# The q projection of the first head group joins the K projection between the modulation units, taken in six shares of channels

## The reference, cut to what matters

```
mod   = silu(c)     @ ada_w + ada_b      # (6 * 2048); mod_c the same with c_ctx
h     = rms_norm(x)   * norm1_g * (1 + sc1)  + sh1
hc    = rms_norm(ctx) * norm1_g * (1 + csc1) + csh1
proj  = h  @ w_in          # qa, ka, va, qb, kb, vb, gates; each of qa..vb is 1024 columns
projc = hc @ w_in          # of which keys and values are used
```

## Time and profile before

| | |
|---|---|
| median of 3 runs | 1735.7 us (1734.41 to 1738.12) |
| the profiled execution | 1735.94 us, span 1734.3 us |
| TensorE busy | 97% of the span |
| VectorE, ScalarE, GpSimd busy | 62%, 43%, 6% |
| mean transfer rate | 214 GB/s; about 387 GB/s until 130 us |
| TensorE's clock | 0.7 in the first of 40 slices of the span, full in the others |

### The profile page before, as it was taken

The page is one execution under the profiler, slowest core; times in us unless marked ns, Lnnn a source line. Parts: engine busy times, 40 slices in busy tenths (PEclk is TensorE's granted clock), DMA queues, the critical chain, the costliest instruction groups (busy, mean ns, idle before and its releaser), DMA issues.

```text
span 1734.3 us, 23809 instructions
## 1 busy us (share of the span) xinstructions
PE 1683.1 (97%) x8800; PEld 1376.4 (79%) x8800; DVE 1082.6 (62%) x1351; ACT 752.3 (43%) x960; POOL 108.7 (6%) x161
## 2 busy tenths in 40 slices
PE   4999999999999999999999999999999999999996
PEld 1468888888888678888888788888888888888885
DVE  1338777768796675554555666666666666655556
ACT  2233222623222564444444555555555555444444
POOL 0002222122121000000000000000000000000000
PEclk7999999999999999999999999999999999999999
DMA  9999988369695127566565566666666665555551
GB/s 354 386 387 334 305 298 283 77 234 333 227 323 193 51 83 261 191 190 192 188 242 190 150 184 193 186 190 191 186 191 189 187 191 186 191 194 193 194 193 62
DMA packets 161237, 371.53 MB, mean 214 GB/s; under 512 B 11607, under 2 KB 12359, under 8 KB 160022
## 3 DMA queue, kind: packets, MB, share of 16 engines
q1 hardware_dynamic: 139808, 291.98, 51.9%
q0 software_dynamic: 20144, 74.22, 12.6%
q10 hardware_dynamic: 1222, 4.47, 0.6%
HBM read 368.43 MB, written 2.21 MB: 214 GB/s over the span
## 4 chain that ended last, share of the span: by engine, by line
PE 92%; DMA 4%; DVE 2%; ACT 1%; issue 1%; SPq 0%; DVEq 0%; POOL 0%; ACTq 0%
PE ps L1838 21%; PE ps L1837 10%; PE ps L1847 10%; PE ps L1849 10%; PE ps L1848 10%; PE ps L2224 4%; PE ps L2225 4%; PE ps L2223 4%; PE ps L1762 3%; DMA raw<-in_ada_w 3%; PE ps L1764 3%; PE ps L1763 3%; PE ps L1834 1%; PE ps L1754 1%; PE ps L1916 1%; PE ps L1898 1%
## 5 line engine op out<-in xcount | busy, mean ns | idle before, releaser
L1127 DVE TENSOR_TENSOR w_lo<-raw,w_hi 128x1024 fp32r<-128x1024 f32 x480 | 584.8, 1224 | 432.9 <-ACT w_hi L669 432.5
L669 ACT CAST w_hi<-raw 128x1024 fp32r<-128x1024 f32 x480 | 503.4, 1050 | 771.3 <-PE ps L1849 273.8
L1838 PE MATMUL ps<-h2T,w_hi 128*128 128x512 f32 x1320 | 463.2, 394 | 0.0
L1837 PE MATMUL ps<-h2T,w_lo 128*128 128x256 f32 x1320 | 366.9, 278 | 0.0
L1838 PEld LDWEIGHTS ps<-h2T,w_hi 128*128 128x128 f32 x1320 | 247.9, 188 | 53.6
L1837 PEld LDWEIGHTS ps<-h2T,w_lo 128*128 128x128 f32 x1320 | 248.4, 188 | 4.2
L1847 PE MATMUL ps<-w_hi,hT 128*128 128x512 f32 x512 | 202.5, 395 | 0.0
L1849 PE MATMUL ps<-w_hi,hT 128*128 128x512 f32 x512 | 199.4, 390 | 0.0
L1848 PE MATMUL ps<-w_lo,hT 128*128 128x512 f32 x512 | 199.4, 389 | 0.0
L1201 DVE SCALAR_TENSOR_TENSOR ada_acc<-ada_raw,silu_c,ada_acc 128x512 f32<-128x512 f32 x240 | 180.0, 750 | 27.2 <-DMA ada_raw<-in_ada_w 11.5
L2223 PE MATMUL ps<-w_hi,f_hi 128*128 128x512 f32 x352 | 137.0, 389 | 1.0 <-DVE conv_in L1583 1.0
(11 more groups left out here) (224 smaller groups left out, 1917.1 us busy)
## 6 DMA issues: line engine op xcount, KB each, us to landing
raw<-in_ffn_w_up SPq DMA_DIRECT2D x176, 512.0 KB, 3.8
raw<-in_w_in SPq DMA_DIRECT2D x152, 512.0 KB, 4.7
ada_raw<-in_ada_w POOLq DMA_DIRECT2D x128, 512.0 KB, 5.9
raw<-in_ffn_w_down SPq DMA_DIRECT2D x88, 512.0 KB, 4.4
raw<-in_ada_w SPq DMA_DIRECT2D x64, 512.0 KB, 10.7
raw<-in_w_out SPq DMA_DIRECT2D x32, 512.0 KB, 3.9
raw<-in_w_branch_a SPq DMA_DIRECT2D x16, 512.0 KB, 3.7
raw<-in_w_branch_b SPq DMA_DIRECT2D x16, 512.0 KB, 3.6
```

The costliest lines, as they stand in the source:

```text
L669: act.copy(w_hi[:, s % SPLIT_SLOTS, :], raw[:, s, :]).then_inc(hi_ready[s], 1)
L1127: dve.tensor_tensor(w_lo[:, s % SPLIT_SLOTS, :], raw[:, s, :], w_hi[:, s % SPLIT_SLOTS, :], ALU.subtract).then_inc(lo_ready[s], 1)
L1837: pe.matmul(ps[:, b + t, 0:SEQ], w_lo[:, row4(s), at], high(kc), start=False, stop=False)
L1838: mm = pe.matmul(o, w_hi[:, row4(s), at], both(kc), start=False, stop=(kc == KC - 1))
```

## The change

The channels are taken in six shares of 2, 4, 4, 2, 2 and 2 groups. A share of four is as a quarter was: sixteen units, one channel group of rows and 1024 columns each. A share of two is eight units; a unit holds two channel groups of rows and 512 columns (256 of shift, 256 of scale), still 512 KB, but brought by two DMAs whose contiguous runs are 1 KB where they were 2 KB. The number of units stays 64. In a share of two the two channel groups' sums lie in different partitions, and `turn_mod` adds them by a matmul with a small matrix (`pair_sum`, made once on VectorE).

The q weights of job 1 now go through `ada_raw` too: K and q pieces alternate, sixteen in all, fourteen of them placed among the units by `KQ_LOADS`. TensorE works in chunks: a slot has six, four of K (six 512-column matmuls) and two of q (two tiles each, twelve 256-column matmuls; latent tokens only, hi*hi, hi*lo, lo*hi added in one PSUM area instead of two). 36 chunks stand among the units (`CHUNKS`), 12 behind them. The q result needs no addition on VectorE. All token groups are turned in one bank (7), which also takes `turn_mod`. Job 1 is gone from the loops of all engines; its 12 ada steps are spread over jobs 2 to 5 (41, 14, 40, 33). The copy of the K result stands in ScalarE's queue at job 2, slot 2.

```diff
-QUARTERS = 4
-SHARE = KC // QUARTERS
-K_AFTER = (3, 10)
-K_TILES = {(0, 0): (1, 6), (0, 1): (1, 8), (0, 2): (1, 10), (0, 3): (1, 12),
-           (1, 0): (1, 13), (1, 1): (1, 15), (1, 2): (2, 1), (1, 3): (2, 3),
...
+SHARES = (2, 4, 4, 2, 2, 2)
+FIRST_KC = [sum(SHARES[:q]) for q in range(len(SHARES))]
+ROWS_OF = [2 if n == 2 else 1 for n in SHARES]
+UNITS_OF = [KC // n for n in ROWS_OF]
+KQ_LOADS = {(1, 1): 0, (1, 4): 1, (1, 9): 2, (1, 13): 3, (2, 2): 4, (2, 6): 5, (2, 9): 6, (2, 12): 7,
+            (3, 1): 8, (3, 3): 9, (3, 5): 10, (4, 0): 11, (4, 4): 12, (4, 7): 13}
+KQ_CHUNKS = 6
+CHUNKS = {1: (7, 9, 11, 13, 15), 2: (1, 5, 6, 7, 8, 9, 10, 11, 12, 14, 15), 3: (1, 3, 5, 6, 7),
+          4: (0, 1, 2, 3, 4, 5, 6, 7), 5: (0, 1, 2, 3, 4, 5, 6)}
+SPLIT_BEFORE = {1: (2, 3), 2: (6, 7), 4: (12,)}
+SPLIT_BEHIND = {3: (10,), 5: (14,)}
+SPLIT_AFTER = {0: (0,), 1: (1,), 3: (4,), 5: (5,), 7: (8,), 9: (9,), 11: (11,), 12: (13,), 15: (15,)}
-ADA_BANKS = (0, 4, 5, 4)
-MOD_BANK = 6
+ADA_BANKS = [6 * (q > 0) for q in range(len(SHARES))]
+MOD_BANK = 7
+TURN_BANK = 7
-ADA_STEPS = {1: 12, 2: 34, 3: 13, 4: 37, 5: 32, 6: 24, 7: 13, 8: 28, 9: 13, 10: 32, 11: 18}
+ADA_STEPS = {2: 41, 3: 14, 4: 40, 5: 33, 6: 24, 7: 13, 8: 28, 9: 13, 10: 32, 11: 18}
...
 # SyncE, a modulation unit and a weight piece
-                    sp.dma_start(raw[:, n % SLOTS, :].rearrange("p (a n) -> p a n", a=2),
-                                 shift_scale[:, kc, :, GROUP * q:GROUP * (q + 1)]).then_inc(raw_landed[n % SLOTS], 16)
+                    for k in range(ROWS_OF[q]):
+                        sp.dma_start(dst[:, k, :, :], shift_scale[:, ROWS_OF[q] * u + k, :, cols])\
+                            .then_inc(raw_landed[n % SLOTS], 16)
...
+                    if i >= 2:
+                        sp.wait_ge(k_landed[i % 2], 16 * (i // 2))
+                    if i >= ADA_SLOTS:
+                        sp.wait_ge(lo_ready[s - 2], j + 1)
+                    sp.dma_start(ada_raw[:, i % ADA_SLOTS, :, :], w_in_v[:, 2 * s:2 * s + 2, col:col + GROUP])\
+                        .then_inc(k_landed[i % 2], 16)
...
 # TensorE
+            def head_q(s, t):
+                o, row = ps[:, 4 + t // 2, (t % 2) * SEQ:(t % 2 + 1) * SEQ], head_row(1, s)
+                for i in range(2):
+                    kc = 2 * s + i
+                    at = slice(i * GROUP + t * P, i * GROUP + (t + 1) * P)
+                    pe.matmul(o, w_hi[:, row, at], hT[:, 0, 0, kc, :], start=(kc == 0 and t % 2 == 0), stop=False)
+                    pe.matmul(o, w_hi[:, row, at], hT[:, 0, 1, kc, :], start=False, stop=False)
+                    mm = pe.matmul(o, w_lo[:, row, at], hT[:, 0, 0, kc, :], start=False,
+                                   stop=(kc == KC - 1 and t % 2 == 1))
+                return mm
...
+            for _, q, u in ADA_UNITS:
+                unit_ada(q, u)
+                if q and u == 0:
+                    turn_mod(q - 1)
+                for _ in range(CHUNKS.get(q, ()).count(u)):
+                    head_chunk(chunks)
+                    chunks += 1
+                if q:
+                    for n, behind in ((0, 1), (1, 2), (2, 4), (3, 5)):
+                        if u == behind and n < SHARES[q - 1]:
+                            turn_tokens(FIRST_KC[q - 1] + n)
+            last_pair = KQ_CHUNKS * (SLOTS - 1)
+            head_chunk(chunks)
+            turn_mod(len(SHARES) - 1)
+            head_chunk(chunks + 1)
+            turn_tokens(KC - 2)
+            head_chunk(chunks + 2)
+            turn_tokens(KC - 1)
...
-            for j in range(JOB_NA + 1, JOB_DIFF - 1):
+            for j in range(JOB_NA + 2, JOB_DIFF - 1):
                 projection(j)
```

More of the change, by code:

```diff
@@ L588, in load_ada @@
                     if skip_wait and pair < ADA_SLOTS:
-                        pool.wait_ge(lo_ready[SLOTS - ADA_SLOTS + pair], 1)
+                        pool.wait_ge(lo_ready[SLOTS - 2 + pair // 2], pair % 2 + 1)
                     else:
@@ L820, in _ @@
             last = JOB_DIFF - 1
-            for j in range(JOB_NA + 1, JOB_DIFF):
+            for j in range(JOB_NA + 2, JOB_DIFF):
                 for s in range(SLOTS):
@@ L1753, in unit_ada, with products_k @@
                 for n, at in enumerate(PIECE_AT):
+                    kc = u if SHARES[q] == 4 else 2 * u + n // 2
                     mm = pe.matmul(ps[at:at + 32, ADA_BANKS[q], 0:PIECE], c_pair[:, 2 * kc:2 * kc + 32],
-                                   raw[:, slot, n * PIECE:(n + 1) * PIECE], start=(kc == 0), stop=(kc == KC - 1))
+                                   raw[:, slot, n * PIECE:(n + 1) * PIECE], start=(u == 0),
+                                   stop=(u == UNITS_OF[q] - 1))
                 mm.then_inc(ada1_used, 1)
-            def products_k(slot, t, b, kc, i):
+            def products_k(row, t, b, kc, i):
@@ L1768, in unit_k, with head_row @@
+                pe.matmul(o, w_hi[:, row, at], hT[:, :, 1, kc, :], start=False, stop=False)
+                return pe.matmul(o, w_lo[:, row, at], hT[:, :, 0, kc, :], start=False, stop=(kc == KC - 1))
+            def unit_k(s, row, t, b):
                 for i in range(2):
-                    mm = products_k(slot, t, b, 2 * s + i, i)
+                    mm = products_k(row, t, b, 2 * s + i, i)
                 return mm
-            def head_k(s, t):
-                if t == 0:
+            def head_row(j, s):
+                return (2 * s + j) % SPLIT_SLOTS
@@ new lines, in _ @@
+            last_pair = KQ_CHUNKS * (SLOTS - 1)
[5 more added lines that the diff above has]
+            turn_tokens(KC - 1)
+            for n in range(chunks + 3, last_pair):
+                head_chunk(n)
+            take(0, SLOTS - 1)
+            for i in range(2):
+                pe.wait_ge(hT_ready, KC - 1 + i)
+                for t in range(TILES):
+                    mm = products_k(head_row(0, SLOTS - 1), t, 0, KC - 2 + i, i)
@@ L1818, in sum_mod @@
+            mm.then_inc(used[SLOTS - 1], 1)
+            for n in range(last_pair + TILES, last_pair + KQ_CHUNKS):
+                head_chunk(n)
             def sum_mod(g, j):
```

237 lines of the change are left out of this document (122 added, 115 removed), and 4 rows, old and new, of the table K_TILES.

## The result

The changed kernel takes 1740.33 us (median of 8 runs, 1738.25 to 1743.50) against 1736.74 for the kernel before on the same chips (8 runs): a ratio of 1.0022, 95% interval [1.0013, 1.0031]. The spans of the profiled executions are 1738.9 and 1734.3 us. Job 2 starts at 159.50 us instead of 155.14. What is lost is lost in the head.

A forecast was written before the change was run, and what follows sets the result against it. TensorE's own work behind the last transfer it waits for was taken as the bound: landing 66.9 plus 91.2 us puts job 2 at 158.1 against 155.14, +3.0 on 1735.94, so 1738.9 us; range 1735.5 to 1742.5.

The forecast's parts named there:

- The landing at 66.9: Share 2's unit 5 (number 29) lands at 66.9 us with TensorE there for it; no wait for transfers later.
- The work behind unit 29: TensorE's work from 66.9 us to job 2: 90.7 us, with 0.5 added 91.2, so job 2 starts at 158.1.
- the other bound: q chunks' 256-column matmuls at 0.15 us each if weight loads could not keep up: 6 us more over 16 chunks.
- the ledger's shortfall: The work ledger, checked on the kernel before, gave 72.4 us against 72.9 in the rows; 0.5 us was added.
- the stall of the second turn in share 3: With one turning bank, a turn one unit behind another waits for ScalarE's modulation: +0.6 us.
- SyncE's new waits: In the head, waits for `k_landed` and `lo_ready` may issue piece 10 up to 2 us late; cost 0.
- the K copy: Behind the last K chunk, 1.86 us, covered by the two last q chunks; uncovered it would cost up to 2.
- changing over: A chunk among the units pays about 0.2 us; for twelve q chunks among the units +2.4 us.
- VectorE late: Rival: VectorE falls behind in jobs 2 to 5, costing some 5 us, 1744 us; chance 0.20.
- Bound by transfers: Rival: transfers bound the head, job 2 at 147.3 us, 1728.1, or 1732 for half; chance 0.11 including hidden idle time.
- 256-column matmuls by their weight loads: Rival: weight loads limit the q chunks' matmuls, +6 us on the forecast, 1745 us; chance 0.06.
- 1 KB runs as 2 KB ones: Rival: in shares of two, 1 KB packets take as long as 2 KB ones; job 2 at about 185, 1766 us; chance 0.03.

The follow-up runs named there:

- e6b: The kernel before with the six shares alone, q left as job 1, tokens turned two units ahead; job 2 at 159.44 us, ratio 1.0027 to the kernel before.
- e1: The changed kernel with its chunks two at a time from share 2 on; job 2 at 157.65 us, ratio 1.0012 to the kernel before.
- e7: q joined as in the changed kernel, but four shares of four groups and chunks in pairs; job 2 at 154.69 us, ratio 0.9994 to the kernel before.
- e10: The changed kernel with chunks in pairs and one 2 KB-run transfer per unit in shares of two; job 2 at 156.14 us, ratio 0.9997 to the kernel before.
- e11: e7 with ten chunks in share 1, token turns moved and splits placed anew; job 2 at 153.90 us, ratio 0.9990 to the kernel before.
- e8: e7 with the token turns spread and the old slot's chunks between them; job 2 at 157.18 us, ratio 1.0004 to the kernel before.
- e9: e8 with the chunks three at a time; job 2 at 159.48 us, ratio 1.0008 to the kernel before.
- e3b: The changed kernel, units of shares of two by one 128-partition transfer with 2 KB runs, other columns; job 2 at 157.81 us, ratio 1.0013 to the kernel before.

## Why the prediction was right, and where not

**Time and side.** +3.0 us was predicted; it is +4.4 at job 2 and +3.6 at the medians. 1740.33 lies in the forecast's own range (1735.5 to 1742.5) and on the side forecast. The forecast called this "within" 3.5 us of the kernel before; the medians lie 3.6 us apart, just outside that, and the interval of the ratio is clear of 1. The forecast's mechanism, TensorE's own work behind the last transfer that it waits for, is what the trace shows. Of the 1.4 us at job 2 between 158.1 and 159.50, 0.4 were there at unit 29 and 1.0 came in behind it.

**The landings.** 1.53 us was worked out for a unit with 1 KB runs, 1.50 is in the rows. The first unit with a chunk was to land at 43.9 and started at 44.35. The chunk itself came 6.35 us before that of the kernel before and not 7.8, which set a landing against a chunk's start. Unit 29 was to be waited for at 66.9; it started at 67.33 without a wait, because TensorE's last wait was at 55.19. So no transfer was waited for later, as said, but the last one sooner. The landing at 66.9, the base of the sum, set nothing: TensorE's own work did, and that the two lie 0.4 us apart is partly luck. The sum by the rule of the Trainium skill (DMA: Bandwidth & Descriptors, Specifications), 512 B for line rate, would have been 1.4 us lower. The trace doesn't agree: 359 and 354 GB/s for 1 KB runs against 386 for 2 KB.

**The work behind unit 29.** 91.2 us predicted, 92.2 in the rows. The mis-sized terms are small and all on one side:
- The q chunk. 24 matmuls take 2.87 us from 156.63 to 159.50, 0.120 each and not 0.115, so a chunk is 1.44 and not 1.38; a unit with a q chunk takes 2.20 (78.72 to 80.92) and not 2.16. Fourteen of them stand behind unit 29: 0.6 to 0.8 us. Of the two neighbours in the earlier trace rows I had taken the mean with half a 512-column one; 0.12, the row itself, would have been right. The 0.15 of the other bound stands in no row.
- A `turn_mod` of a share of two takes 0.47 (106.13 to 106.60) and not 0.27, behind the loop 0.37 (142.81 to 143.18): four small matmuls for two. Three of them: some 0.5 us.
- Against these 1.1 to 1.3 us stand the 0.5 us that were added for the ledger's shortfall.

A unit with a K chunk takes 2.16 (80.92 to 83.08), the stall of the second turn in share 3 0.59, the last unit stands at 140.75 (about 140), and SyncE's new waits and the K copy cost nothing: as predicted. Behind the loop it took 18.2 us (141.32 to 159.50) for 17.5.

**What the loss was put down to.** The total held; the reason given for the loss did not. The prediction put +2.4 us on changing over for twelve q chunks, and on the shares 0.5 (two `turn_mod`), 0.6 (the stall) and 1.4 (1 KB runs ahead of the first chunk). It concluded that the q products fill gaps worth less than their changes-over. The runs show that they fill gaps worth about as much. With q left out the shares alone lose the same (159.44, e6b), or 1.4 us less when the wait of that order is taken off. With quarters and pairs q costs nothing that these runs can tell (154.69 against 154.53 and 155.14).

The shares cost 3.0 to 4.3 us (e6b against before). With q and pairs on both sides it is 3.0 (157.65 against 154.69, ratios 1.0012 and 0.9994), though e1 and e7 also pair their chunks in different places. Of these 3.0, 1.5 went with one transfer of 2 KB runs for two of 1 KB (157.65 to 156.14 by e10). The remaining 1.5 us are not explained: the ratios of e10 and e7 (0.9997 and 0.9994) don't tell the two apart, and the waits for `mod_rows`, 1.0 us in e10 and none in e7, are 1.0 us in e11 too, which has quarters.

The changes-over are real, but they are a price of single chunks, not of q alone: one cycle of unit and K chunk pays 2.16 - 0.50 - 1.385 = 0.28 us against unbroken rows, a pair of each 3.95 - 1.00 - 2.77 = 0.18. The change has 36 chunks in the loop where before had 24. Pairs gave the changed kernel 0.96 us, 1.57 with 2 KB runs (104.35 to 102.78), and the kernel before 0.6 to 0.9.

**Rivals.** VectorE late: no wait for `w_lo` behind job 2, so it didn't come. Bound by transfers: not behind 55 us. But there they lie close: e1, e8, e9 and e11, which took work from TensorE or moved it, all waited for transfers again, 0.3 to 2.6 us at a time. That is why the pairs, worth 0.37 us each, did not pay in full. 256-column matmuls by their weight loads: 0.120, a seventh of the way from 0.115 to 0.15. 1 KB runs as 2 KB ones: no.

## What to carry to other kernels

Where two limits lie within a few per cent of each other, an edit that relieves one is worth only the distance to the other: read both ledgers along the whole stage, not at one point, before a gain is counted. Count what an edit's *form* costs apart from its idea: here the idea (q beside the modulation) showed no net cost, and the finer shares that were to make room for it brought the loss, part of it by shorter runs in the one stretch that waits for transfers. Compare two executions from the last event that both have alike: of the 1.85 us that the pairs seemed to give, 0.89 stood ahead of the first chunk that they moved. And a total that comes out right does not show that its terms are right: only the runs that did one part alone did.

## What the runs showed of the chip

- Two transfers of 64 partitions with 2 KB runs for one of 128 partitions: 237 GB/s from 100 to 120 us, against 383 for the same runs in one transfer (e3b). The run length is the same, the split makes it. Why it does stays open.
- Runs of 1 KB, in two transfers of 256 KB: 1.50 us for 512 KB against 1.36 for 2 KB runs in one transfer, 10% more.
- 256-column products with a weight load each keep a pace of 0.120 us over 24 in a row, 512-column ones 0.23 (five K chunks from 126.03 to 132.95 before).
- From the start of a token turn to its tokens ready for a product it is 2.9 us (79.80 to 82.74), and turns in a row can start 1.8 us apart. In e7, TensorE, ScalarE and VectorE in order of time:

```profile
79.80 0.66 PE L1761 MATMUL ps<-consts,tokens 128*128 128x128 f32 x4 [0.59 <-ACT modulated L773]
...
80.54 1.02 ACT L773 ACTIVATE modulated<-ps,shift,gain 128x256 f32<-128x256 f32 x2 [0.80 <-issue]
...
81.61 0.66 PE L1761 MATMUL ps<-consts,tokens 128*128 128x128 f32 x4 [0.16 <-ACT modulated L773]
82.05 0.69 DVE L1215 TENSOR_TENSOR hT<-modulated,hT 128x512 fp32r<-128x512 f32 x1
```
